# A transformer and Hyena kernel: the Hyena filter generator moved beside the output projection, and the stick-breaking softplus fed to TensorE as two fp32r parts

## The reference, cut to what matters

```python
log_beta = jax.nn.log_sigmoid(z)                      # z = q k^T, causal
log_one_minus = jnp.where(causal, log_beta - z, 0.0)  # = -softplus(z)
rem = lax.cumsum(log_one_minus, axis=3, reverse=True) - log_one_minus
w = jnp.where(causal, jnp.exp(log_beta + rem), 0.0)
out = w @ v
```

```python
hid = jnp.sin(freq * (emb @ w1 + b1))
hid = jnp.sin(freq * (hid @ w2 + b2))
h = (hid @ w3 + b3).reshape(L, 2, 2, 1024) * decay
kern = concat([fwd, 0, reversed bwd]);  kern = kern / sum(abs(kern))
k_f = jnp.fft.rfft(kern, axis=0)
```

## Time and profile before

| | |
|---|---|
| median of 3 runs | 2398.31 us (2396.13 to 2398.44) |
| the profiled execution's own time | 2393.65 us |
| its span, first to last instruction | 2391.6 us |
| mean granted TensorE clock | 0.952 of full |
| stick-breaking loop, first Abs to last weights | 809.62 to 940.35 us |
| output projection wo2, last matmul to first filter matmul | 1845.9 to 1872.2 us |
| filter loop to the input projection | 1872.2 to 2000.8 us |

### The profile page before, as it was taken

How to read it: one execution, slowest core, us unless ns; L and a number is a source line. 1 busy time by engine, 2 the same in 40 slices (tenths; PEclk the granted TensorE clock), 3 DMA queues, 4 the chain that set the end, 5 groups by cost and what they waited for, 6 DMA issues and landing times. The chain is left out here.

```text
span 2391.6 us, 27416 instructions
## 1 busy us (share of the span) xinstructions
PE 2222.0 (93%) x10853; PEld 1602.6 (67%) x10853; DVE 1224.3 (51%) x2281; ACT 728.4 (30%) x1002; POOL 665.2 (28%) x397
## 2 busy tenths in 40 slices
PE   7859899999999889999999989899999788999888
PEld 6858688888778656688888754347764335886653
DVE  8561499984330132378860121567761584225871
ACT  3422332321330454332321311444441121332210
POOL 6514344445431200344444300010000332441000
PEclk9979899999999999899999989989999579999999
DMA  4032244434312100244433301110001122332101
GB/s 172 6 55 88 82 139 150 141 119 130 114 60 98 61 1 10 88 141 145 146 110 97 146 29 66 44 35 1 1 1 50 75 88 97 97 97 97 71 18 70
DMA packets 49999, 193.65 MB, mean 81 GB/s; under 512 B 9161, under 2 KB 9337, under 8 KB 44143
## 3 DMA queue, kind: packets, MB, share of 16 engines
q1 hardware_dynamic: 35712, 140.14, 18.5%
q0 software_dynamic: 10432, 50.59, 5.8%
q10 hardware_dynamic: 3728, 1.18, 0.3%
HBM read 179.04 MB, written 10.49 MB: 79 GB/s over the span
## 5 line engine op out<-in xcount | busy, mean ns | idle before, releaser
L1407 POOL TENSOR_TENSOR w_lo<-raw,w_hi 128x1024 fp32r<-128x1024 f32 (+1 forms) x208 | 494.2, 2377 | 872.4 <-ACT w_hi L1065 872.2
L575 PE MATMUL psum<-h_hi,w_hi 128*128 128x512 f32 x1280 | 514.0, 402 | 10.8 <-ACT h_hi L1072 5.5
L576 PE MATMUL psum<-h_hi,w_lo 128*128 128x512 f32 x1280 | 506.1, 395 | 0.0
L1065 ACT ACTIVATE w_hi<-raw 128x1024 fp32r<-128x1024 f32 (+1 forms) x208 | 216.4, 1041 | 640.8 <-PE psum L580 428.5
L580 PE MATMUL psum<-h_lo,w_hi 128*128 128x512 f32 x1280 | 317.7, 391 | 0.0
L575 PEld LDWEIGHTS psum<-h_hi,w_hi 128*128 128x128 f32 x1280 | 243.6, 190 | 77.8 <-ACT h_hi L1072 14.1
L576 PEld LDWEIGHTS psum<-h_hi,w_lo 128*128 128x128 f32 x1280 | 244.9, 191 | 48.0
L580 PEld LDWEIGHTS psum<-h_lo,w_hi 128*128 128x128 f32 x1280 | 241.8, 189 | 50.4
L445 PE MATMUL psum<-big,ring 128*128 128x512 f32 x480 | 208.6, 594 | 0.0
L445 PEld LDWEIGHTS psum<-big,ring 128*128 128x128 f32 x480 | 91.3, 191 | 113.3 <-issue 112.4
L622 PE MATMUL psum<-f_hi,w_hi 128*128 128x512 f32 x352 | 137.8, 392 | 0.0
(11 more groups left out here) (347 smaller groups left out, 3181.5 us busy)
## 6 DMA issues: line engine op xcount, KB each, us to landing
raw<-in_ffn_w_up SPq DMA_DIRECT2D x88, 512.0 KB, 3.6
raw<-in_ffn_w_down SPq DMA_DIRECT2D x32, 512.0 KB, 3.6
raw<-in_hy_in SPq DMA_DIRECT2D x32, 512.0 KB, 3.5
ffn_buf<-in_ada_w POOLq DMA_DIRECT2D x20, 512.0 KB, 5.0
sq<-in_ada_w POOLq DMA_DIRECT2D x20, 512.0 KB, 5.1
raw<-in_ssm_w_glu SPq DMA_DIRECT2D x16, 512.0 KB, 3.7
spec<-big POOLq DMA_DIRECT2D x8, 1024.0 KB, 4.1
big<-spec POOLq DMA_DIRECT2D x8, 1024.0 KB, 5.1
```

The source lines that it names most:

```text
L575: pe.matmul(o, hi[:, k, :], HHI[:, k, :], start=k == 0, stop=False)
L576: pe.matmul(o, lo[:, k, :], HHI[:, k, :], start=False, stop=False)
L1065: act.activation(w_hi[:, (n % 2) * HALF:(n % 2) * HALF + w], raw[:, (n % 4) * HALF:(n % 4) * HALF + w], ACT.Copy).then_inc(S["w_hi"], 1)
L1407: pool.tensor_tensor(w_lo[:, at:at + w], raw[:, (n % 4) * HALF:(n % 4) * HALF + w], w_hi[:, at:at + w].bitcast(F32), ALU.subtract).then_in ...
```

## The change

The line numbers are those of the kernel before. Two parts of the program change, and they share nothing but the file.

In the stick-breaking loop VectorE computes softplus in place in `LN_`, rounds it to fp32r in `SPH` and puts the rest in `SPL`, first for columns 512 to 1280 and then for 0 to 512; both buffers are single. `cumulate` multiplies both parts by fp32r copies of the two constant matrices, ten matmuls for each part, and the three sums of 128 columns are gone. ACT makes Ln in two pieces, and `weights(h-1)` goes ahead of Ln of head h.

In the Hyena part the two first layers run between tiles of wo2 (after tiles 1 and 4), their loads and those of `w3` and `decay` are issued earlier, the spread of the inverse root comes after `filters(0)`, and the odd tiles of the transform are copied by ACT (`spectrum_odd`). Buffers move so that nothing of the softmax attention that is still live is overwritten.

```diff
-        SP = [bigv(16384 + ZW * i, ZW) for i in range(2)]
+        SPH, SPL = (f_lo[:, at:at + ZW] for at in (5120, 5120 + ZW))
+        NEGTRI, NEGONES = (f_lo[:, at:at + P] for at in (10240, 10240 + P))
+        SP_PARTS = ((512, ZW), (0, 512))
...
+        HID_BESIDE = (1, 4)
...
             def cumulate(h):
-                for i in range(4):
-                    pe.matmul(zblk(o, i), mat("negtri"), sp[:, ZAT[i]:ZAT[i] + L - P * i], ...)
-                later = [(2, P, ...), (1, P, ...), (0, P, ...), (1, 2 * P, sums...), (0, 2 * P, sums...)]
-                pe.wait_ge(S["sp_sum"], 3 * (h + 1))
-                for i, lo, v in later:
-                    m = pe.matmul(zblk(o, i, lo)[:, 0:w], mat("negones"), v, ...)
+                def tri(i, sp):
+                    pe.matmul(zblk(o, i), NEGTRI, sp[:, ZAT[i]:ZAT[i] + L - P * i], ...)
+                def later(i, sp):
+                    for j in range(i + 1, 4):
+                        pe.matmul(zblk(o, i, P * (j - i)), NEGONES, sp[:, ZAT[j]:ZAT[j] + L - P * j], ...)
+                for ready, sp in ((S["sp_hi"], SPH), (S["sp_lo"], SPL)):
+                    pe.wait_ge(ready, 2 * h + 1)
+                    for i in (1, 3, 2):
+                        tri(i, sp)
+                        later(i, sp)
+                pe.wait_ge(S["sp_hi"], 2 * h + 2)
+                later(0, SPH)
+                tri(0, SPH)
+                later(0, SPL)
+                pe.wait_ge(S["sp_lo"], 2 * h + 2)
+                m = pe.matmul(zblk(o, 0), NEGTRI, SPL[:, 0:L], ...)
...
+            def hidden(m):      # TensorE, beside=hidden of wo2
+                if m not in HID_BESIDE:
+                    return
+                i_ = HID_BESIDE.index(m)
+                o = take(pe, ("hid", i_))
+                pe.wait_ge(*((S["hid_ready"], 1) if i_ else (S["hid_in"], 32)))
+                w, h = (small[0:64, 64:128], HID[0][0:64, :]) if i_ else (small[0:33, 0:64], EMB[0:33, :])
+                fills(pe.matmul(o[0:64, :], w, h, start=True, stop=True), ("hid", i_))
...
             norm("nw1")
-            pe.wait_ge(S["hid_in"], 48)
-            (the matmuls of hid 0 and hid 1, each after its wait)
             pe.wait_ge(S["hid_ready"], 2)
             pe.wait_ge(S["hid_one"], 1)
-            pe.wait_ge(S["dft_in"], 16)
+            pe.wait_ge(S["w3_in"], 16)
...
             filters(0)
+            spread("nw1")
+            pe.wait_ge(S["dft_in"], 16)
...
             def softplus(h):    # ACT
                 step(act.activation(LN_[b], LN_[b], ACT.Exp, scale=-1.0))
-                own()
-                act.activation(LN_[b], LN_[b], ACT.Ln, bias=1.0).then_inc(S["ln_ready"], 1)
                 if h >= 1:
                     weights(h - 1)
+                own()
+                for lo, hi in SP_PARTS:
+                    act.activation(LN_[b][:, lo:hi], LN_[b][:, lo:hi], ACT.Ln, bias=1.0).then_inc(S["ln_ready"], 1)
...
+            def spectrum_odd(u, f):    # ACT
+                act.wait_ge(S["spec_used"], 2 * u + f)
+                for a in (1, 3):
+                    evac(("fs", u, f, a), scr[:, (a // 2) * 512:(a // 2) * 512 + 512])
...
                 if u:           # after the eight Abs of turn u
+                    spectrum_odd(u - 1, 0)
                     split_rows("nw1", NW1_ROWS[u - 1])
+                    spectrum_odd(u - 1, 1)
+            spectrum_odd(3, 0)
+            spectrum_odd(3, 1)
...
+            pool.wait_ge(S["roped"], 15)
+            pool.dma_start(small[0:64, 0:128], A["hy_w12"][:, :])
+            pool.dma_start(EMB[0:33, :], A["emb"][:, :])
+            pool.memset(HID[1][64:65, :], 1.0)
+            pool.wait_ge(*full(("o2", 15)))
+            pool.dma_start(W3[0:65, :], A["hy_w3"][:, :])
+            pool.dma_start(DEC[:, :, :], A["decay"][:, :, :])
             for t in range(8):
                 pool.wait_ge(*full(("wo2", t)))
-            pool.wait_ge(S["x_ready"], 40)
-            (hy_w12, emb, hy_w3 loaded here; after dft: decay, the norm's wait, the memset)
             pool.dma_start(DFT[:, :], A["dft"][:, :])
...
             for h in range(HEADS + 2):      # DVE
                 if h < HEADS:
-                    STT(sp, z, 0.0, LN_[h % 2], ALU.max, ALU.add).then_inc(S["sp_raw"], 1)
-                    (three TT of 128 columns into sums)
+                    if h:
+                        dve.wait_ge(S["cum_done"], h)
+                    for q, (lo, hi) in enumerate(SP_PARTS):
+                        n = 2 * h + q + 1
+                        dve.wait_ge(S["ln_ready"], n)
+                        z, sp = ps(("z", h), 3).rearrange("p b n -> p (b n)")[:, lo:hi], LN_[h % 2][:, lo:hi]
+                        STT(sp, z, 0.0, sp, ALU.max, ALU.add).then_inc(S["sp_raw"], 1)
+                        dve.wait_ge(S["sp_raw"], n)
+                        dve.tensor_copy(SPH[:, lo:hi], sp).then_inc(S["sp_hi"], 1)
+                        dve.wait_ge(S["sp_hi"], n)
+                        TT(SPL[:, lo:hi], sp, SPH[:, lo:hi].bitcast(F32), ALU.subtract).then_inc(S["sp_lo"], 1)
...
+            def hidden_arg(i_):      # DVE: the eight steps as before, on other buffers
+            def hidden(m):
+                if m - 1 in HID_BESIDE:
+                    hidden_arg(HID_BESIDE.index(m - 1))
+            add_x("wo2", lambda m: adac(0, 2, m), beside=hidden)
...
             decay(0)
+            dve.wait_ge(*full(("rb", "nw1")))
+            keep_r("nw1")
...
-                    for a in (1, 3):
-                        dve.wait_ge(*full(ks[a]))
-                        frees(dve.tensor_copy(ev[a // 2], ps(ks[a])), ks[a])
```

More of the change, by code:

```diff
@@ L121, in build @@
             "ada_sums", "masks_ready", "ca_ready", "bbz_ready", "x_states", "k_diag", "t_zero", "t_in", "t_in_pool",
-            "conv_base", "silu_ready", "kz_zero", "ln_ready", "sp_raw", "sp_sum", "cum_done", "s_lat",
+            "conv_base", "silu_ready", "kz_zero", "ln_ready", "sp_raw", "cum_done", "s_lat",
             "rn_ready",
+            "w3_in",
+            "neg_ready", "sp_hi", "sp_lo",
             "cols_in", "bc_in",
@@ L417, in norm @@
                 fills(i, ("norm", name))
-                if name in WIDE_NORMS and name not in ("mix0", "ctx"):
+                if name in WIDE_NORMS and name not in ("mix0", "ctx", "nw1"):
                     spread(name)
@@ L870, in o2_wait @@
                 pe.wait_ge(*free(("o2", 2 * k + 1)))
-            lin("wo2", A["attn_w_out"], 4, lambda k: G2[:, k, :], wait=o2_wait, x_base=32)
-            norm("nw1")
-            pe.wait_ge(S["hid_in"], 48)
[L876 to L880, removed]
+            def hidden(m):
[6 more added lines that the diff above has]
+                fills(pe.matmul(o[0:64, :], w, h, start=True, stop=True), ("hid", i_))
+            lin("wo2", A["attn_w_out"], 4, lambda k: G2[:, k, :], wait=o2_wait, x_base=32, beside=hidden)
+            norm("nw1")
             pe.wait_ge(S["hid_ready"], 2)
             pe.wait_ge(S["hid_one"], 1)
-            pe.wait_ge(S["dft_in"], 16)
+            pe.wait_ge(S["w3_in"], 16)
             def filter_norm(u):
@@ L897, in filters @@
                     c0 = (2 * (u // 2) + d) * 1024 + (u % 2) * 512
-                    fills(pe.matmul(o, HID[0:65, 1, t * P:(t + 1) * P], W3[0:65, c0:c0 + 512], start=True, stop=True),
+                    fills(pe.matmul(o, HID[1][0:65, t * P:(t + 1) * P], W3[0:65, c0:c0 + 512], start=True, stop=True),
                           key)
             filters(0)
+            spread("nw1")
+            pe.wait_ge(S["dft_in"], 16)
             for u in range(4):
@@ L1276, in _ @@
                     sm_exp(n)
+            for i in range(2):
+                act.wait_ge(S["arg_ready"], 2 + i)
+                act.activation(HID[i][0:64, :], ARG[0:64, :], ACT.Sin).then_inc(S["hid_ready"], 1)
+            act.wait_ge(S["hid_ready"], 2)
             norm("nw1", ready=x_wait)
             n_x[0] += 8
-            for i in range(2):
-                act.wait_ge(S["arg_ready"], 2 + i)
-                act.activation(HID[0:64, i, :], ARG[0:64, :], ACT.Sin).then_inc(S["hid_ready"], 1)
+            def spectrum_odd(u, f):
+                act.wait_ge(S["spec_used"], 2 * u + f)
+                for a in (1, 3):
+                    evac(("fs", u, f, a), scr[:, (a // 2) * 512:(a // 2) * 512 + 512])
             n0 = HALVES_AT["hy"]
@@ L1969, in _ @@
                     sm_gate((n - 8) // 4)
-            add_x("wo2", lambda m: adac(0, 2, m))
-            inv_rms("nw1")
-            keep_r("nw1")
-            dve.wait_ge(*free(("rb", "nw1")))
-            rms_nw1 = rms[:, 0:L]
-            for i_ in range(2):
+            def hidden_arg(i_):
                 dve.wait_ge(*full(("hid", i_)))
                 a = ARG[0:64, :]
-                kq = scr[0:64, 0:L]
+                kq = sq[0:64, 1024:1536]
                 frees(TS(a, ps(("hid", i_))[0:64, :], col("fw", 1 + i_, 64), col("fw", 0, 64), ALU.add, ALU.mult),
```

56 lines of the change are left out of this document (23 added, 33 removed).

## The result

The changed kernel takes 2354.41 us (median of 4 runs, 2353.00 to 2356.61); the kernel before took 2398.32 beside it. The ratio is 0.982, 95% interval 0.9807 to 0.9833: 43.9 us faster, where 37.5 were forecast. The profiled execution took 2354.87 us, 38.8 less than that of before.

The account below looks back on a forecast made before the run. TensorE, busy 93% of the span, was taken as the bound. Savings of 23.0 + 6.5 + 8.0 = 37.5 us off the 2398.31 us median gave 2360.8 us (2356.2 for the profiled execution), range 2346 to 2380.

Parts of the forecast that it names:

- part 1: Start of the Hyena filters, from the norm's matmuls to the first transform: 55.3 us become 32.3, saving 23.0 us.
- part 2: Odd-tile copies moved to ACT in the filter turns and behind them: saves 6.5 us, lower bound 1.3.
- part 3: Stick-breaking loop: two heads take 15.4 us instead of 16.46, saving 8 us over 7.5 pairs.
- the second place: In time order, the later place touched: the end of the output projection, where the filters start; the prediction lists it first.
- The filters stay at the full clock: Rival at the filters' start: TensorE no longer idles before them, so 33 us saved instead of 23, total 2350.8; chance 0.17.
- So it starts full and falls on the way: Step on the clock under filters(0): full at first, then lower, so its eight tiles take 10.1 us.
- The rule that the prediction cited: Keep TensorE continuously busy and the full clock is granted; by it the sum would be 47.5 us.
- The small terms of part 1: At the filters' start: first layers' two matmuls cost 1.7 us, their chains hide under wo2, the DFT load lands in time.
- The stall at the third projection tile: Input projection: split_lo 4.1 us sooner cuts a 3.9 us wait to about 0.5 and avoids the low clock; 5.2 us.
- The view that f = 0 gains nothing: First half of a filter turn: ACT, paced by GpSimd's sums, copies when VectorE did, so moving copies saves nothing.
- the 128-column rival: Stick-breaking loop: fp32r matmuls of 128 columns cost 0.24 like float32, so -2 us instead of +8, total 2370.8; chance 0.16.
- The slower rival: The stick-breaking loop falls to the lower clock, 16 heads lose 74 us, total 2443; chance 0.03.

Follow-up runs that it names:

- hyena_only: The kernel before with everything of the change except the new stick-breaking loop, so the Hyena part alone: 2360.61 us, ratio 0.9845.
- after_dft_first: The changed kernel with TensorE waiting for the DFT tables ahead of turn 0's first filter matmul instead of the first transform: 2367.34 us, ratio 0.9873.
- after_mixed: The changed kernel with the odd tiles of the first half of turns 0 to 2 copied by VectorE, the others by ScalarE: 2356.19 us, ratio 0.9826.
- before_again: The kernel before, unchanged, run and profiled once more as a control: 2397.6 us, ratio 1.0004.
- after_ln_first: The changed kernel with ScalarE taking the previous head's weights after the logarithm again in the stick-breaking loop: 2370.43 us, ratio 0.9884.

## Why the prediction was right, and where it was off

The time, 2354.4, lies inside 2346 to 2380 and 6.4 below the forecast. By the profiled executions it is 2354.9 against 2356.2. The mechanisms were the right ones, and the sizes erred both ways.

- **The near hit is partly luck.** Between the profiled executions part 1 gave 7.0 more than forecast, part 2 gave 0.9 more, and part 3 some 3 less; what was lost ahead of the loop (1.6) and between it and the second place (2.6) took most of the rest. By the medians the 6.4 us that the forecast fell short are about part 1's miss.
- **Part 1, forecast 23.0, measured 32.0 less the hidden layers' 2.0, so 30.** The rival came true: "The filters stay at the full clock". The failed step is "So it starts full and falls on the way". I read it from "28 us of nothing but filters never brought it back", a row about getting a lost clock back, and used it for keeping one. The runs tell the two apart. Straight behind dense work the 65-row filters kept the full clock in the changed kernel and in `hyena_only`; behind a gap of 5.9 us they did not. The rule that the prediction cited from the Trainium skill, "TensorE: Matmul & The Clock Gate", section "Why this matters for your kernels", held here for keeping the clock. For getting it back it did not hold for these matmuls: 27.68 us of them without a break stayed at 0.50 in before, as the prediction said. The rival's own 33 us, worked out from VectorE's chain, was off by one term: `even_odd(0)` at 8.80 for 6.3, GpSimd's sums now being beside all of it (in `after_dft_first`, where only the last of them was, it took 5.03).
- **The small terms of part 1 held.** The first layers' matmuls cost 1.0 us each (forecast 1.7 for both), and their chains lay under wo2. The DFT load was no hindrance.
- **Part 2, forecast 6.5, measured 7.4.** The stall at the third projection tile went as forecast (4.6 us, forecast 5.2); ahead of it the stretch gave 2.8 where 1.3 were forecast. Undoing the copies alone cost 5.8. The view that f = 0 gains nothing held, and `after_mixed` shows why in a sharper way than I had argued: ScalarE and TensorE come within 0.1 us of each other there.
- **Part 3, forecast 8.0, measured 7.7 to 9.0 by its own run, 4.4 by the two traces up to the matmul behind the loop.** The steady pair is 15.20 us (forecast 15.4), and the 128-column rival is out: the six matmuls of one part, 1280 columns, are issued in 0.77 us (857.84 to 858.61, forecast 0.7), and the last of them, of 128 columns, is followed 0.06 us after its start, where the sum had 0.107. Missed was the start of the loop at the half clock, some 3 us against the trace of before, and it comes with the new loop in each of its ten traces. The old loop had it at its first running sums alone, in two traces of four (`before_again`: 0.76 over 813 to 820), and never under the third head's scores. The execution of before that was profiled had none of it; its 2393.65 us are under all timed runs of before but one (2392.94), which is part of what the traces lack against the runs. Why the new loop loses the clock there stays open: TensorE's waits ahead, 2.58 and 1.33 us, are no longer than the old loop's 2.85 and 1.33.
- **The slower rival** did not come, but `after_ln_first`, one order apart, has it in part.

## What to carry to other kernels

A lower clock is two questions, whether the stretch loses the clock and whether it can win it back, and a row that answers one says nothing of the other: look at what ran ahead of it. Where a wait ends, look for the second engine that would have ended it a moment later, before taking the named one out of the way. And before giving work to an idle GpSimd, look for VectorE's additions from SBUF beside it, for they may be on the path.

## What the runs showed of the hardware

- The number of rows in a float32 matmul had a say in the granted clock. Over 65 rows 27.68 us of unbroken matmuls stayed at 0.50; over 128 rows, same columns and same place, the full clock came back some 4 us in. With 65 rows the second four filter tiles of a turn took 6.1 to 7.2 us behind TensorE's wait of 1.2 to 2.8 us, in every trace; with 128 rows they took 3.70 behind waits of 1.2 to 2.1. In the filter stage of all fourteen traces the clock came back during 128-row matmuls or, once, 0.3 us after they had given way to 65-row ones (`after_dft_first`). Straight behind dense work, with no wait, the 65-row filters kept the full clock. Why the rows count isn't shown.
- VectorE's eight additions from SBUF to SBUF took 4.9 us alone and 8.8 to 9.5 beside GpSimd's two-operand work; those that read PSUM took 0.60 to 0.69 each either way.
- With a wait of TensorE of 2.33 us in each pair of heads (`after_ln_first`) the clock fell to 0.50 seven times within the loop; with one of 1.32 us (changed kernel) it stayed full in the steady loop.
